# Turning sliding attention's keys and taking its scores earlier, and one low part in halves, in a two-layer encoder on one core

## The reference

```
h = rms_norm(x, mix_norm_pre[l])
proj = h @ w_in[l]
lru_x, lru_g, sq, sk, sv, dq, dk, dv = jnp.split(proj, list(IN_OFFSETS), axis=-1)
y_lru = rglru_mixer(lru_x, lru_g, ...)            # recurrence * gelu(lru_g)
y_swa = swa_mixer(sq, sk, sv, swa_sinks[l], rel_bias)   # 4 heads, 2 key heads, window 128
y_diff = diff_mixer(dq, dk, dv, lam, lam_init, diff_head_gain[l], rel_bias)
y = jnp.concatenate([y_lru, y_swa, y_diff], axis=-1) @ w_out[l]
x = x + rms_norm(y, mix_norm_post[l])
```

## Time and profile before

| | |
|---|---|
| median of 3 runs | 954.49 us (954.47 to 954.55) |
| profiled execution, its own time | 954.41 us |
| its span, first to last instruction | 952.7 us |
| TensorE matmuls busy | 941.0 us, 99% of the span |
| weight loads (PEld) busy | 813.4 us, 85% |
| VectorE busy | 678.0 us, 71% |
| ScalarE busy | 528.4 us, 55% |
| GpSimd busy | 25.6 us, 3% |

### The profile page before, as it was taken

How to read it: one execution, slowest core, us unless ns; L and a number is a source line. 1 busy time by engine, 2 the same in 40 slices (tenths; PEclk the granted TensorE clock), 3 DMA queues, 4 the chain that set the end, 5 groups by cost and what they waited for, 6 DMA issues and landing times.

```text
span 952.7 us, 12886 instructions
## 1 busy us (share of the span) xinstructions
PE 941.0 (99%) x5177; PEld 813.4 (85%) x5177; DVE 678.0 (71%) x1001; ACT 528.4 (55%) x704; POOL 25.6 (3%) x45
## 2 busy tenths in 40 slices
PE   8999999999999999999999999999999999999997
PEld 7888888888987888888888888888889888888886
DVE  6967867788788856656788666658878887665664
ACT  6635544558776645445565454445697575544442
POOL 0400000000000012000000000000000000000000
PEclk9999999999999999999999999999999999999999
DMA  9688565366325767655466656555653356565541
GB/s 310 210 264 280 183 203 188 135 207 233 133 89 159 259 201 210 206 181 185 161 210 218 200 188 207 180 185 198 195 175 133 114 196 201 193 203 177 189 165 45
DMA packets 131770, 180.22 MB, mean 189 GB/s; under 512 B 4104, under 2 KB 115224, under 8 KB 131712
## 3 DMA queue, kind: packets, MB, share of 16 engines
q1 hardware_dynamic: 129504, 175.65, 56.4%
q0 software_dynamic: 2192, 3.76, 1.8%
q10 hardware_dynamic: 16, 0.00, 0.0%
HBM read 178.33 MB, written 2.63 MB: 190 GB/s over the span
## 4 chain that ended last, share of the span: by engine, by line
PE 90%; DVE 6%; ACT 2%; issue 1%; DVEq 0%
PE UP L438 31%; PE Y L465 25%; PE UP L443 16%; PE UP L755 4%; PE Y L453 4%; PE UP L760 2%; DVE wlo L1178 1%; PE UP L768 1%; PE Y L519 1%; PE Y L512 1%; PE Y L514 1%; ACT junk L874 1%; PE Y L545 1%; DVE logit L1484 1%; PE UP L477 1%
## 5 line engine op out<-in xcount | busy, mean ns | idle before, releaser
L1178 DVE TENSOR_TENSOR wlo<-raw,whi 128x2048 fp32r<-128x2048 f32 x152 | 347.9, 2290 | 123.1 <-ACT whi L857 123.1
L857 ACT ACTIVATE whi<-raw 128x2048 fp32r<-128x2048 f32 x159 | 304.1, 1913 | 92.3 <-DMA raw<-in_ffn_w_gate 69.2
L438 PE MATMUL UP<-xT,whi 128*128 128x512 f32 x1280 | 304.9, 390 | 0.0
L438 PEld LDWEIGHTS UP<-xT,whi 128*128 128x128 f32 x1280 | 237.4, 188 | 47.5
L465 PE MATMUL Y<-whi,yT 128*128 128x512 f32 x736 | 206.5, 391 | 0.0
L443 PEld LDWEIGHTS UP<-xT,wlo 128*128 128x128 f32 x1280 | 164.1, 191 | 6.2
L443 PE MATMUL UP<-xT,wlo 128*128 128x256 f32 x1280 | 166.0, 283 | 0.0
L465 PEld LDWEIGHTS Y<-whi,yT 128*128 128x128 f32 x736 | 135.2, 188 | 25.6
L465 PE MATMUL Y<-wlo,yT 128*128 128x512 f32 x368 | 113.6, 390 | 0.0
L969 ACT ACTIVATE gate_small<-UP 128x512 f32<-128x512 f32 x40 | 23.8, 596 | 110.0 <-PE UP L443 109.9
L465 PEld LDWEIGHTS Y<-wlo,yT 128*128 128x128 f32 x368 | 69.1, 188 | 14.8
(11 more groups left out here) (225 smaller groups left out, 883.6 us busy)
## 6 DMA issues: line engine op xcount, KB each, us to landing
raw<-in_ffn_w_up SPq DMA_DIRECT2D x44, 1024.0 KB, 5.4
raw<-in_ffn_w_down SPq DMA_DIRECT2D x44, 1024.0 KB, 5.0
raw<-in_ffn_w_gate SPq DMA_DIRECT2D x43, 1024.0 KB, 5.3
raw<-in_w_in SPq DMA_DIRECT2D x20, 1024.0 KB, 5.3
raw<-in_w_out SPq DMA_DIRECT2D x8, 1024.0 KB, 4.9
gains<-in_ffn_norm_post SPq DMA_DIRECT2D x4, 512.0 KB, 5.8
shift_scratch<-shift_rows POOLq DMA_DIRECT2D x1, 1536.0 KB, 14.7
gains<-in_ffn_norm_pre SPq DMA_DIRECT2D x3, 512.0 KB, 5.9
```

Source lines behind the costliest of these rows:

```text
L438: nc.tensor.matmul(bank(UP, b + c), h[:, kt, c * P:c * P + P], xT[:, kt, :, :].rearrange("p h s -> p (h s)"), start=kt == 0, stop=False, s ...
L857: A.activation(whi[:, k % RING, :], raw[:, k % RING, :], ACT.Copy).then_inc(hi_ready, 1)
L1178: V.tensor_tensor(wlo[:, k % RING, :], raw[:, k % RING, :], whi[:, k % RING, :].bitcast(F32), ALU.subtract).then_inc(lo_ready, 1)
```

## The change

In both mixers TensorE turns the keys ahead of the gate's first tile and takes sliding attention's scores right behind that tile, ahead of the turned weights of JOB_B. ScalarE copies the turned keys ahead of unit 11's high part. VectorE does the low part of unit 12 in two halves of 1024 columns: the first where the whole stood, the second behind the gelu's cube.

```diff
--- before.py
+++ after.py
@@ -801,11 +801,11 @@
                 in_tile(U_SWKV, 0)
                 in_tile(U_SWKV, 1)
                 turn_output(l, JOB_A)
+                turn_keys(l)
                 in_tile(U_LRU_G, 0)
-                turn_keys(l)
+                scores(l, JOB_SWA)
                 pe.wait_ge(mix_lo, l * OUT_UNITS + 1)
                 turn_weights(l, JOB_B)
-                scores(l, JOB_SWA)
                 in_tile(U_LRU_G, 1)
                 values(l, JOB_B)
 
@@ -1119,9 +1119,9 @@
                 tile(U_SWKV, 0)
                 tile(U_SWKV, 1)
                 output_hi(JOB_A)
+                keys_copy()
                 sp(11)
                 tile(U_LRU_G, 0)
-                keys_copy()
                 copy_turned(JOB_B)
                 sp(12)
 
@@ -1613,10 +1613,11 @@
                 sp(10)
                 sp(11)
                 softmax_logits(JOB_SWA)
-                sp(12)
+                split_part(stage_unit(s, 12), 0, 1024)
                 job_output(JOB_B)
                 softmax_weights(JOB_SWA)
                 gelu_cube()
+                split_part(stage_unit(s, 12), 1024, 2048)
                 job_lo(JOB_B, 2)
                 gelu_gate()
                 output_lo(3, 0, lru_out[:, :, :])
```

## The result

The changed kernel took **956.28 us** (median of 22 runs), the kernel before 954.85 (22 runs): a ratio of 1.0013 with a 95% interval of 1.0007 to 1.0019. It is slower by some 1.4 us (the medians lie 1.43 apart, the lowest times, 955.84 and 954.33, 1.51): clear of zero with so many runs, and inside the 0.2% that was called no difference. One of the 22 runs of the changed kernel took 1903.82 us and stands outside the ratio; nothing here shows what befell it. The profiled execution took 956.44 us, with a span of 954.7.

The account below looks back on a forecast made before the run. TensorE, busy for all but about 11 us, was taken to bound the kernel. Each mixer would lose 0.67 us at the second out unit: 2 x 0.67 = +1.34 us on the 954.49 median, giving 955.8; range 954.0 to 956.9.

Parts of the forecast that it names:

- The keys' wait, 0.44: TensorE, ahead of the gate's first tile: a new 0.44 us stall while the keys wait for ScalarE's copy L1026.
- The old stall gone, 0.25: TensorE, before the scores: the 0.25 us wait for the copied keys `swk` disappears.
- the two stalls: TensorE's waits for `swk` (0.25) and `att` (0.36), in both mixers; together they could give back 1.2 us.
- ScalarE, 0.72: ScalarE's queue: turned weights copied 1.92 us later; idle time swallows part, so sliding attention's exponentials start 0.72 later.
- VectorE's wait for the square: VectorE before L1527: idles about 1.3 us for ScalarE's square; L1527 starts 0.21 later than before.
- The half in front of L1537, 1.13 and 0.80 late: VectorE behind the gelu's cube: the second half takes a 1.13 us step, making low output L1537 0.80 later.
- The out unit, 0.67: TensorE's second out unit waits for L1537 and starts 0.67 us late in each mixer.
- Nothing lost or regained behind it: Behind the second out unit, VectorE's next chores have room, so no more time is lost or regained.
- it works as meant: Rival: ScalarE's square comes by 265.9, both stalls of 0.61 go, none new stays: 953.3 us; chance 0.13.
- slower than can be missed: Rival: ScalarE bounds the stretch; first sliding-attention exponential after 264.03 instead of 263.74; at 264.2, 956.8 us; chance 0.17.

Follow-up runs that it names:

- The last kernel: The change with keys inside the gate's first tile, ScalarE's unit 12 high part before its turned-weight copies, second half behind the gelu's gate: 953.62 us against 954.48.
- high part ahead: The whole change, with ScalarE making unit 12's high part ahead of its copies of the second group's turned weights: 955.13 us against 954.69 for the kernel before.
- halves alone: The kernel before with only the change's halved low of unit 12 on VectorE; keys and scores stay: 954.75 us against 954.69.
- the order alone: The change with the low of unit 12 whole again in its old place, keys and scores early: 955.06 us against 954.69 for the kernel before.
- change with keys inside: The whole change, with keys turned inside the gate's first tile behind two of its eight blocks: 955.09 us against 954.60 for the kernel before.

## Why the prediction was right, point by point

The forecast was +1.34 us, the medians moved by 1.43 and the two stretches by 1.52 (0.74 and 0.78). In absolute numbers 955.8 was forecast and 956.28 measured: the kernel before itself read 954.85 in this comparison, where the forecast counted from 954.49. The mechanism is the one that was forecast, and each part of it was taken away by itself. The size is less exact than 1.34 beside 1.43 looks: by the stretches 0.09 on average is missing in each mixer, and errors on the way cancelled in part.

- *The keys' wait, 0.44.* Measured 0.44 (0.80 less 0.36), and it names L1026. Right.
- *The old stall gone, 0.25.* Mis-sized: it was 0.11. I took the pace of transposes among themselves for the distance to matmuls of another shape. So all that the two stalls could give back was 2 x (0.11 + 0.36) = 0.9 us and not 1.2. (The last kernel won 0.54 in each mixer, 0.07 more than 0.47: 0.03 ahead of the gate's second tile, which starts at 5.96, and 0.03 between `att`'s transposes and the last ones of L705, 1.80 instead of 1.83 now that the former start without a wait.) The same step was priced at nothing in the change: the scores start 0.21 behind the last L768 (259.09 to 259.30), where L694 followed it after 0.12 (257.73 to 257.85 in the kernel before), and with 0.02 from the rest the gate's second tile was 0.30 late, not 0.19.
- *ScalarE, 0.72.* The copy of the turned weights came 2.08 later, not 1.92, yet the exponentials 0.76: the step from the high part to an exponential is 1.81 (262.47 to 264.28), where I had put in its whole length of 1.92. Two errors, of 0.16 and 0.11, that nearly cancel: this is luck.
- *VectorE's wait for the square.* Forecast some 1.3, measured 1.24; L1527 was 0.24 late against 0.21.
- *The half in front of L1537, 1.13 and 0.80 late.* Measured 1.13 (271.82 to 272.95) and 0.78. The overlap that the earlier trace rows show at a whole low holds for a half. The Trainium skill's page "VectorE: DVE Perf Modes", section "The DRAIN you can't avoid", says that the next operation does not start until the pipe is empty, and by that alone the step would have been 1.22; the section adds that an operation which is not held starts earlier, which the prediction left out. In this trace the next operation started 0.09 before the half's end.
- *The out unit, 0.67.* Measured 0.76. L1537 ended at 273.64 and the matmul started at 273.79: 0.15 from end to start where I had 0.04. This is the term of the sum that was mis-sized: 0.11 too little, less the 0.02 above, is the 0.09 that is missing in each mixer.
- *Nothing lost or regained behind it.* L453 was 0.74 late, the same as the out unit less 0.02.

The rival "it works as meant" needed ScalarE's square in time. The run with the high part ahead shows it was one exchange of lines from that, and even then the second half kept the gain from arriving. The rival "slower than can be missed" had its point at the first exponential, 0.29 beyond my value; that instruction came 0.04 beyond it. The parts do not add: halves alone cost 0.01, the order alone 0.23, both 0.74, because behind the late square L1527 starts at 12.09 with and without the halves: the order took away the 0.53 that the first half gains there, and left what the second half costs.

## What to carry to other kernels

When a step is taken forward on one engine, ask what its successor on the other engines stands behind: here scores taken early gave VectorE nothing and put ScalarE's next 1.9 us of independent work behind a wait. Work that is split to free a critical step must have its second part in a real hole of the queue, behind the next thing that somebody waits for; two steps further back turned the same split from nothing into 0.38 us per mixer. And a step that waits belongs inside the work that covers its wait, not in front of it.

## What the runs showed of the hardware that I had not expected

- The distance from two transposes to matmuls that use half of the rows was 0.31 us with nothing to wait for, in two kernels, against 0.18 at the pace of transposes among themselves (0.09 each). Four transposes in front of a matmul that uses all rows, into another bank, kept that pace (0.35).
- A matmul released by VectorE's low output started 0.15 us behind its end, in the change and in the three other kernels where it waited (halves alone, high part ahead, change with keys inside); transposes released by `att` or `swv` and scores released by `swk` started 0.05 to 0.06 behind theirs, in the kernel before and in the change.
- ScalarE's exponential started 1.81 us behind the start of a high part of 1.91, 0.10 before its end.
